# Seven products from the fourth pair on, and refilled stage borders, in a two-layer hybrid decoder trunk

## Chip, cores and metric

One Trainium2 chip, one core. The metric is the device time of one execution in microseconds (us), median of several runs.

## What is computed

The trunk has two layers. In each, x is normalized (RMSNorm), goes through a mixer (gated DeltaNet in layer 0, GLA in layer 1) and is added back, then through a gated feed-forward with a causal convolution of three taps, all in float32. The change is in the feed-forward and at its borders:

```python
D_MODEL, SEQ, D_FF, FFN_CONV = 1024, 1024, 2816, 3

def conv_glu_ffn(h, w_up, conv_w, w_down):
    u = causal_depthwise_conv(h @ w_up, conv_w)
    gate, val = jnp.split(u, 2, axis=-1)
    return (jax.nn.silu(gate) * val) @ w_down

for layer in range(2):
    hn = rms_norm(x, mix_pre_norm[layer])
    m = ...
    x = x + rms_norm(m, mix_post_norm[layer])
    f = conv_glu_ffn(rms_norm(x, ffn_pre_norm[layer]), ffn_w_up[layer],
                     ffn_conv_w[layer], ffn_w_down[layer])
    x = x + rms_norm(f, ffn_post_norm[layer])
```

## The kernel before

Every float32 matrix is split in a high part (rounded to the type that TensorE multiplies at full rate, fp32r) and a low part (the rest). A product is three matmuls: high by high, high by low, low by high (`product3`, lines 81 to 83). ScalarE makes the high parts by a copy, GpSimd the low parts of weights by a subtraction, VectorE most low parts of activations.

**The up projection.** The 2816 hidden units are 22 tiles of 128. A pair is one gate tile and one value tile of the same units, tiles 2p and 2p+1, each 128 units by 1024 tokens. The tokens are taken in two halves, near (0 to 511) and far. The first `PLAIN` = 4 pairs are made directly: per tile 2 halves x 8 blocks of the inner dimension x 3 matmuls of 128x512. The 18 others are made by seven products of half size (Strassen's scheme in Winograd's form, `first_products` for the first such pair and `seven_products`), 7 x 4 x 3 matmuls. Their operands are sums of weight quarters (`sums`, made by GpSimd's `combine`, their lows by `low`) and of token quarters (`t1`, `t2`, `t4`, and a fourth that overwrites the far half of x's first rows; made by VectorE).

**The token sums** have eight pieces, numbered 0 to 7: `first_difference`, `second`, `fourth` for c = 0 and 1, and `third_difference` for c = 0 and 1. For each, VectorE makes the sum in two or three instructions over SBUF (lines 824 to 843), ScalarE its high part (`token_sum_high`, line 616) and VectorE its low part (`token_sum_low`, line 848). Their scratch space is the tile `kept` and `spare`, the same memory in which ScalarE later keeps products of a seven-product pair (`keep`, line 653). So the first `keep` waits for all eight lows (`s_tlo` 8). The third sum's pieces overwrite x's far half and wait for `s_b12`, the last use of those tokens.

**Order.** There is no scheduler: each engine runs its own list in program order, and semaphores tie them. Per pair, ScalarE scales the gate out of PSUM (`scaled_gate`, line 626), VectorE adds the two other taps (`conv`, lines 876 and 881), ScalarE applies silu (642) and scales the value (637), VectorE convolves it and multiplies (`activated`, 887). PE may write a PSUM tile again only when its convolution is done (`ready`). For the down projection VectorE also makes four row sums of the first two pairs' hidden units (`row_sum`, 898 to 905) in the tile `sums`; SyncE stores them, and only then (`s_rstore`) may GpSimd put weight sums there:

```python
for s in s_rstore:
    pool.wait_ge(s, 16)
for pair in range(PLAIN, FT):
    operands(pair)
```

The keep of the first product stands in ScalarE's list behind all work of the last plain pair, and the second operand's product waits for it (`s_kept` 1):

```python
pe.wait_ge(s_tlo, 6)
pe.wait_ge(s_kept, 1)
quarter_product(p, S2, chain_ps, t2_hi, t2_lo, False, False)
```

**The borders.** The mixer's end (`mixer_tail`) turns and splits the new x tile by tile; between the last tiles PE already makes the near half of the feed-forward's tile 0 (`half_product`). Then all engines meet, the stage's semaphores are cleared (`clear`, line 71), all meet again (line 72), and the feed-forward's block begins. SyncE first loads the taps, then raw tiles. The feed-forward's own end does the same towards the next mixer (`lead`), with its last down steps, norms (`m_normed`, `x_normed`), deviations and turns listed by step number.

## Time and profile before

| | |
|---|---|
| median of 3 runs | 2616.05 us |
| lowest, highest | 2615.96, 2616.66 us |
| profiled execution | 2617.55 us |
| its span on the core | 2616.1 us |
| mean granted TensorE clock | 0.993 of full |

The profile is one execution of the whole program. PE is TensorE, DVE VectorE, ACT ScalarE, POOL GpSimd, SP SyncE. An engine's name with a q is its queue. A wait is put down to the instruction whose semaphore came last. The layer 0 feed-forward lies between 794 and 1463 us, that of layer 1 from 1966 us to the end.

### The profile page before, as it was taken

How to read it: one execution, taken by the hardware profiler on the slowest of the kernel's cores; microseconds unless marked ns; L12 is line 12 of the kernel's file. 1: busy time of each engine (PE TensorE's matmuls, PEld its weight loads, DVE VectorE, ACT ScalarE, POOL GpSimd, SP SyncE). 2: the span in 40 equal slices, each digit the busy share in tenths (PEclk: the TensorE clock that was granted, in tenths of full speed). 3: DMA queues.
4: the chain of work that ended last, by engine and by line, in shares of the span. 5: the costliest groups of instructions: out<-in, count | busy, mean ns of one | idle time of the engine just before them, and what ended most of it. 6: DMA issues, size and time to landing. Idle time of an engine off the chain costs nothing. (4 is left out here: it accounts for less than half of the span.)

```text
span 2616.1 us, 34535 instructions
## 1 busy us (share of the span) xinstructions
PE 2539.9 (97%) x12557; PEld 2105.9 (80%) x12557; DVE 1645.8 (63%) x1797; ACT 1189.6 (45%) x1738; POOL 1312.4 (50%) x843
## 2 busy tenths in 40 slices
PE   7899999999899999999999899999999999999998
PEld 5788888888777788888887688788877888888887
DVE  5677666777167767667328657557457766676327
ACT  6445445545443444444446434434533444444444
POOL 2454335353502778775667111111503778785767
PEclk9999999999899999999999999999999999999999
DMA  3234444334443233324765211111523223224666
GB/s 136 61 115 138 128 124 133 84 119 118 127 144 118 77 109 98 112 93 140 235 226 192 83 35 47 32 48 35 160 104 110 90 96 114 97 101 155 220 216 217
DMA packets 123392, 313.06 MB, mean 120 GB/s; under 512 B 13473, under 2 KB 27361, under 8 KB 119937
## 3 DMA queue, kind: packets, MB, share of 16 engines
q1 hardware_dynamic: 119936, 288.31, 32.6%
q0 software_dynamic: 3328, 23.07, 4.6%
q8 instruction: 78, 1.28, 0.2%
q14 instruction: 50, 0.40, 0.0%
HBM read 247.33 MB, written 110.13 MB: 137 GB/s over the span
## 5 line engine op out<-in xcount | busy, mean ns | idle before, releaser
L527 POOL TENSOR_TENSOR f_wlo<-f_raw,f_whi 128x512 fp32r<-128x512 f32 x154 | 265.5, 1732 | 137.9 <-ACT f_whi L610 137.8
L484 POOL TENSOR_TENSOR f_wlo<-f_raw,f_whi 128x512 fp32r<-128x512 f32 (+1 forms) x122 | 198.0, 1624 | 235.5 <-ACT f_whi L579 235.5
L912 DVE TENSOR_TENSOR f_wlo<-f_raw,f_whi 128x512 fp32r<-128x512 f32 x154 | 149.5, 981 | 174.7 <-ACT f_whi L610 174.7
L610 ACT ACTIVATE f_whi<-f_raw 128x1024 fp32r<-128x1024 f32 x154 | 162.7, 1059 | 202.8 <-PE f_value L83 100.9
L484 POOL TENSOR_TENSOR f_wlo<-f_sums,f_whi 128x512 fp32r<-128x512 f32 x144 | 193.1, 1363 | 37.3 <-ACT f_whi L579 37.3
L81 PE MATMUL f_value<-x_hi,f_whi 128*128 128x512 f32 x416 | 162.9, 392 | 3.4 <-POOL f_wlo L484 1.9
L82 PE MATMUL f_value<-x_lo,f_whi 128*128 128x512 f32 x416 | 162.6, 391 | 0.0
L83 PE MATMUL f_value<-x_hi,f_wlo 128*128 128x512 f32 x416 | 162.5, 391 | 0.0
L653 ACT ACTIVATE f_kept<-f_part 128x512 f32<-128x512 f32 x108 | 64.5, 597 | 162.0 <-PE f_part L83 158.0
L2004 POOL TENSOR_TENSOR g_wlo_first<-g_raw_first,g_whi_first 128x1024 fp32r<-128x1024 f32 x15 | 36.7, 2445 | 183.2 <-ACT g_whi_first L2097 183.2
L579 ACT ACTIVATE f_whi<-f_sums 128x512 fp32r<-128x512 f32 x144 | 86.0, 623 | 89.3 <-POOL f_sums L490 89.3
L81 PE MATMUL f_value<-f_whi 128*128 128x512 f32 x308 | 120.9, 393 | 2.8 <-ACT f_acc L676 2.4
L3027 POOL TENSOR_TENSOR l_wlo<-l_raw,l_whi 128x1024 fp32r<-128x1024 f32 x12 | 29.6, 2469 | 183.5 <-ACT l_whi L3056 183.5
L83 PE MATMUL f_value<-f_whi,f_wlo 128*128 128x512 f32 x308 | 120.6, 392 | 0.0
L82 PE MATMUL f_value<-f_wlo,f_whi 128*128 128x512 f32 x308 | 120.4, 391 | 0.0
L81 PE MATMUL banks<-x_hi,g_whi_first 128*128 128x512 f32 x256 | 110.0, 430 | 3.9 <-POOL g_wlo_first L2004 3.9
L83 PE MATMUL f_part<-x_hi,f_wlo 128*128 128x512 f32 x288 | 112.5, 391 | 0.0
L82 PE MATMUL f_part<-x_lo,f_whi 128*128 128x512 f32 x288 | 112.5, 391 | 0.0
L81 PE MATMUL f_part<-x_hi,f_whi 128*128 128x512 f32 x288 | 112.5, 391 | 0.0
L81 PE MATMUL banks<-x_hi,g_whi 128*128 128x512 f32 x256 | 109.0, 426 | 0.0
L83 PE MATMUL banks<-x_hi,g_wlo_first 128*128 128x512 f32 x256 | 101.1, 395 | 0.0
L82 PE MATMUL banks<-x_lo,g_whi_first 128*128 128x512 f32 x256 | 100.9, 394 | 0.0
(566 smaller groups left out, 7814.3 us busy)
## 6 DMA issues: line engine op xcount, KB each, us to landing
f_raw<-in_ffn_w_up SPq DMA_DIRECT2D x88, 512.0 KB, 3.8
f_raw<-operands_of SPq DMA_DIRECT2D x154, 256.0 KB, 2.8
f_raw<-w_sums SPq DMA_DIRECT2D x88, 256.0 KB, 3.0
w_sums<-in_ffn_w_down POOLq DMA_DIRECT2D x28, 768.0 KB, 8.4
f_raw<-in_ffn_w_down SPq DMA_DIRECT2D x66, 256.0 KB, 4.4
operands_of<-f_hid SPq DMA_DIRECT2D x22, 512.0 KB, 2.8
w_sums<-in_ffn_w_down SPq DMA_DIRECT2D x14, 768.0 KB, 7.8
w_sums<-w_sums SPq DMA_DIRECT2D x14, 768.0 KB, 6.7
```

The source lines that it names most:

```text
L81: pe.matmul(out, w_hi, x_hi, start=first, stop=False, skip_group_check=read_between)
L82: pe.matmul(out, w_hi, x_lo, start=False, stop=False, skip_group_check=read_between)
L83: return pe.matmul(out, w_lo, x_hi, start=False, stop=last, skip_group_check=read_between)
L484: pool.tensor_tensor(part_of(w_lo, k), source, part_of(w_hi, k).bitcast(F32), ALU.subtract) \
L527: pool.tensor_tensor(step_part(w_lo, more_lo, d)[:, far], source[:, far], step_part(w_hi, more_hi, d)[:, far].bitcast(F32), ALU.subtract). ...
L579: act.activation(part_of(w_hi, k), source, ACT.Copy).then_inc(s_hi, 1)
L610: act.activation(step_part(w_hi, more_hi, d)[:, :], (raw + [last_raw])[r][:, :], ACT.Copy).then_inc(s_hi, 1)
L653: act.activation(out, chain_ps, ACT.Copy).then_inc(s_kept, 1)
L912: dve.tensor_tensor(step_part(w_lo, more_lo, d)[:, near], source[:, near], plain32(step_part(w_hi, more_hi, d)[:, near]), ALU.subtract).th ...
L2004: pool.tensor_tensor(w_lo[s][:, :], raw[s][:, :], w_hi[s][:, :].bitcast(F32), ALU.subtract) \
L3027: pool.tensor_tensor(w_lo[s][:, :], raw[s][:, :], w_hi[s][:, :].bitcast(F32), ALU.subtract) \
```

## The change

1. `PLAIN` is 3: the fourth pair of each up projection is made by seven products too. The eight pieces of the token sums are made within three plain pairs. Both pieces of the third sum now come in the last plain pair.
2. Tile 1 of each up projection: VectorE makes the low part of its far columns, at the head of its list, and GpSimd that of the near ones. Its raw load is issued ahead of the taps.
3. At the mixers' ends `half_product` is cut into pieces around the last turn, the last one behind the last turned tile. Towards the next mixer it is cut likewise, and the order of the last norms, deviations and turns is another.
4. GpSimd clears no semaphores any more; the longest runs go to SyncE first.
5. In the first mixer's end one weight's high part comes a place later.

```diff
@@ -24,7 +24,7 @@
 FFN_SLOTS = 5
-PLAIN = 4
+PLAIN = 3
 TEMP_OF = (0, 1, 2, 0, 1, 2, 0, 2)
@@ -59,7 +59,7 @@
     def clear():
-        engines = (nc.sync, nc.gpsimd, nc.scalar, nc.vector)
+        engines = (nc.sync, nc.scalar, nc.vector)
         numbers = sorted(s.num for s in made)
@@ -67,7 +67,7 @@
                 first = n
-        for n, run in enumerate(runs):
+        for n, run in enumerate(sorted(runs, key=len, reverse=True)):
             engines[n % len(engines)].sem_clear(run)
@@ -112,9 +112,10 @@
-    def half_product(self, pe):
-        pe.wait_ge(self.s_lo, 1)
-        for kt in range(KT):
+    def half_product(self, pe, tiles):
+        for kt in tiles:
+            if kt == 0:
+                pe.wait_ge(self.s_lo, 1)
             f = slice(kt * P, (kt + 1) * P)
@@ -371,6 +373,8 @@
                 sp.wait_ge(s_lo, raw_released(n - FFN_RAWS))
+            if n == FFN_RAWS + 1:
+                sp.wait_ge(s_value_low, 1)
             sp.dma_start(raw[n % FFN_RAWS][:, :], w_up[layer, n // 2 + n % 2 * FT]).then_inc(s_raw[n % FFN_RAWS], 16)
@@ -416,8 +420,9 @@
+        load(1)
         sp.dma_start(taps[:, :, :], conv_w[layer]).then_inc(s_taps, 16)
-        for n in range(1, 6):
+        for n in range(2, 6):
             load(n)
@@ -430,7 +435,7 @@
                 store_row(R_F, 1)
-            if p >= PLAIN:
+            elif p > PLAIN:
                 for kind, i in ((R_F, p // 2), (R_G, p // 2 - 1)) if p % 2 else ((R_D, p // 2 - 1), (R_S, p // 2 - 1)):
@@ -514,7 +519,10 @@
-        for n in range(1, 2 * PLAIN):
+        pool.wait_ge(s_hi, 2)
+        pool.tensor_tensor(part_of(w_lo, 1)[:, near], raw[1][:, near], part_of(w_hi, 1)[:, near].bitcast(F32),
+                           ALU.subtract).then_inc(s_lo, 1)
+        for n in range(2, 2 * PLAIN):
             low(n, raw[n % FFN_RAWS][:, :])
@@ -725,14 +733,15 @@
             elif p == 1:
-                token_sum_high(1, t2_hi[:, 0:2, :])
                 token_sum_high(2, t4_hi[:, 0:2, :])
-            elif p == 2:
                 token_sum_high(3, t1_hi[:, 2:4, :])
-                token_sum_high(4, t2_hi[:, 2:4, :])
             if p < PLAIN - 1:
...
                 high(2 * p + 3)
+                if p == 0:
+                    token_sum_high(1, t2_hi[:, 0:2, :])
+                else:
+                    token_sum_high(4, t2_hi[:, 2:4, :])
             else:
@@ -784,10 +793,10 @@
                 near_deviation(near_m)
-            near_x = {SEVENTH + 4: 0, SEVENTH + 6: 1, SEVENTH + 9: 2, FOURTH + 1: 3}.get(d)
+            near_x = {SEVENTH + 4: 0, SEVENTH + 6: 1, FOURTH: 2, FOURTH + 2: 3}.get(d)
             if near_x is not None:
                 x_deviation(near_x)
-            near_high = {SEVENTH + 8: 0, FOURTH + 2: 1, FOURTH + 3: 2, FOURTH + 4: 3}.get(d)
+            near_high = {SEVENTH + 8: 0, FOURTH + 1: 1, FOURTH + 4: 2, FOURTH + 5: 3}.get(d)
             if near_high is not None:
@@ -803,10 +812,10 @@
         far_deviation(7)
+        x_deviation(6)
         x_high(5)
-        x_deviation(6)
+        x_deviation(7)
         x_high(6)
-        x_deviation(7)
         x_high(7)
@@ -928,11 +937,10 @@
         def rows_of(q):
-            if q == PLAIN:
-                row_sum(R_F, q // 2 - 1)
             if q % 2:
                 row_sum(R_F, q // 2)
-                row_sum(R_G, q // 2 - 1)
+                if q > PLAIN:
+                    row_sum(R_G, q // 2 - 1)
             else:
@@ -988,6 +996,9 @@
+        dve.wait_ge(s_hi, 2)
+        dve.tensor_tensor(part_of(w_lo, 1)[:, far], raw[1][:, far], plain32(part_of(w_hi, 1)[:, far]), ALU.subtract) \
+            .then_inc(s_value_low, 1)
         dve.wait_ge(s_taps, 16)
@@ -995,24 +1006,23 @@
             elif p == 1:
+                fourth_low(0)
+                first_difference(1)
+                first_low(1)
+            else:
+                fourth_low(1)
+                third_difference(0)
+                third_low(0)
+                third_difference(1)
+                third_low(1)
+            conv(2 * p, gate_ps, gate)
+            if p == 0:
                 second_low(0)
                 fourth(0)
-                fourth_low(0)
-            elif p == 2:
-                first_low(1)
+            elif p == 1:
                 second(1)
...
                 fourth(1)
-            else:
-                fourth_low(1)
-                third_difference(1)
-                third_low(0)
-                third_low(1)
-            conv(2 * p, gate_ps, gate)
-            if p == 1:
-                first_difference(1)
-            if p == 2:
-                third_difference(0)
             conv(2 * p + 1, value_ps[p % 2], hid[p % 2])
@@ -1068,11 +1078,11 @@
         left_gain(7)
+        m_normed(7)
+        x_normed(6)
         x_low(5)
-        x_normed(6)
-        m_normed(7)
+        x_normed(7)
         x_low(6)
-        x_normed(7)
         x_low(7)
@@ -1087,8 +1097,10 @@
             pe.wait_ge(s_lo, n + 1)
+            if n == 1:
+                pe.wait_ge(s_value_low, 1)
             if n >= 2:
-                pe.wait_ge(s_conv, n - 1)
+                pe.wait_ge(s_conv, n - 3 if n % 2 and n > 4 else n - 1)
@@ -1220,7 +1232,7 @@
             last.then_inc(s_prod, 1)
-            t = {SEVENTH + 7: 0, FOURTH: 1, FOURTH + 1: 2, FOURTH + 3: 3}.get(d)
+            t = {SEVENTH + 7: 0, FOURTH: 1, FOURTH + 3: 2, FOURTH + 4: 3}.get(d)
             if t is not None:
@@ -1228,16 +1240,19 @@
         held(3)
+        turn(5)
         if lead is not None:
...
             lead.near_logits(pe, range(KT))
-        turn(5)
-        if lead is not None:
-            lead.half_product(pe, range(0, KT // 2))
+            lead.half_product(pe, range(0, 2))
         turn(6)
         if lead is not None:
-            lead.half_product(pe, range(KT // 2, KT))
+            lead.half_product(pe, range(2, 5))
         turn(7)
+        if lead is not None:
+            lead.half_product(pe, range(5, 6))
+            pe.wait_ge(s_free, NT)
+            lead.half_product(pe, range(6, KT))
@@ -1708,8 +1723,13 @@
             pe.wait_ge(s_free, max(place(t) for t in range(NT // 2)) + 1)
-            follows.half_product(pe)
+            follows.half_product(pe, range(0, 5))
+            pe.wait_ge(s_xn, NT)
+            follows.half_product(pe, range(5, 6))
             turn(NT - 1)
+            follows.half_product(pe, range(6, 7))
+            pe.wait_ge(s_free, NT)
+            follows.half_product(pe, range(7, 8))
@@ -2235,10 +2255,11 @@
                 else:
-                    for kt_ in range(2, 5):
+                    for kt_ in range(2, 4):
                         ScalarTail.weight(act, kt_)
...
                 if final(h):
+                    ScalarTail.weight(act, 4)
                     ScalarTail.mixed_tile(act, 0)
```

VectorE's list at the start of layer 0's block (`f_kept` and `f_spare` are the scratch, `f_t1lo` the low of the first sum, `f_gate` and `f_hid` what the convolutions write), before:

```order
L824 TENSOR_TENSOR f_kept<-x_hi 128x1024
L825 TENSOR_TENSOR f_kept<-x_lo 128x1024
L827 TENSOR_TENSOR f_kept<-f_kept 128x1024
L848 TENSOR_TENSOR f_t1lo<-f_kept,f_t1hi 128x1024
L841 TENSOR_TENSOR f_kept<-x_hi,f_kept 128x1024
L843 TENSOR_TENSOR f_kept<-f_kept,x_lo 128x1024
L876 SCALAR_TENSOR_TENSOR f_gate<-banks,f_taps,f_gate 128x1023
L881 SCALAR_TENSOR_TENSOR f_gate<-banks,f_taps,f_gate 128x1022
L876 SCALAR_TENSOR_TENSOR f_hid<-f_value,f_taps,f_hid 128x1023
L881 SCALAR_TENSOR_TENSOR f_hid<-f_value,f_taps,f_hid 128x1022
```

and in the change:

```order
L1000 TENSOR_TENSOR f_wlo<-f_raw_4201,f_whi 128x512
L833 TENSOR_TENSOR f_kept<-x_hi 128x1024
L834 TENSOR_TENSOR f_kept<-x_lo 128x1024
L836 TENSOR_TENSOR f_kept<-f_kept 128x1024
L857 TENSOR_TENSOR f_t1lo<-f_kept,f_t1hi 128x1024
L850 TENSOR_TENSOR f_kept<-x_hi,f_kept 128x1024
L852 TENSOR_TENSOR f_kept<-f_kept,x_lo 128x1024
L885 SCALAR_TENSOR_TENSOR f_gate<-banks,f_taps,f_gate 128x1023
L890 SCALAR_TENSOR_TENSOR f_gate<-banks,f_taps,f_gate 128x1022
L857 TENSOR_TENSOR f_t2lo<-f_kept,f_t2hi 128x1024
L850 TENSOR_TENSOR f_spare<-x_hi,f_kept 128x1024
L852 TENSOR_TENSOR f_spare<-f_spare,x_lo 128x1024
```

A half low of tile 1 stands at the head, and the second sum's low and the fourth sum come ahead of the value's convolution.

VectorE from the row sums on (`f_sums`) to the next convolution of a gate, before:

```order
L898 TENSOR_TENSOR f_sums<-f_hid 128x512
L900 TENSOR_TENSOR f_sums<-f_hid 128x512
L902 SCALAR_TENSOR_TENSOR f_sums<-f_sums,f_hid 128x512
L905 SCALAR_TENSOR_TENSOR f_sums<-f_sums,f_hid 128x512
L848 TENSOR_TENSOR f_t1lo<-f_kept,f_t1hi 128x1024
L841 TENSOR_TENSOR f_kept<-x_hi,f_kept 128x1024
L843 TENSOR_TENSOR f_kept<-f_kept,x_lo 128x1024
L848 TENSOR_TENSOR f_t2lo<-f_kept,f_t2hi 128x1024
L841 TENSOR_TENSOR f_spare<-x_hi,f_kept 128x1024
L843 TENSOR_TENSOR f_spare<-f_spare,x_lo 128x1024
L876 SCALAR_TENSOR_TENSOR f_gate<-banks,f_taps,f_gate 128x1023
L881 SCALAR_TENSOR_TENSOR f_gate<-banks,f_taps,f_gate 128x1022
```

and in the change:

```order
L911 SCALAR_TENSOR_TENSOR f_sums<-f_sums,f_hid 128x512
L914 SCALAR_TENSOR_TENSOR f_sums<-f_sums,f_hid 128x512
L857 TENSOR_TENSOR f_t4lo<-f_spare,f_t4hi 128x1024
L833 TENSOR_TENSOR f_kept<-x_hi 128x1024
L834 TENSOR_TENSOR f_kept<-x_lo 128x1024
L836 TENSOR_TENSOR f_kept<-f_kept 128x1024
L857 TENSOR_TENSOR x_lo<-f_kept,x_hi 128x2x512
L833 TENSOR_TENSOR f_spare<-x_hi 128x1024
L834 TENSOR_TENSOR f_kept<-x_lo 128x1024
L836 TENSOR_TENSOR f_spare<-f_spare,f_kept 128x1024
L857 TENSOR_TENSOR x_lo<-f_spare,x_hi 128x2x512
L885 SCALAR_TENSOR_TENSOR f_gate<-banks,f_taps,f_gate 128x1023
```

Before, a whole plain pair, the fourth, still follows these rows. In the change the rows (from the third row sum on) are the last plain pair's, with the seventh and the eighth piece (lows into `x_lo`) ahead of its convolution.

ScalarE in the change from the highs of the first seven-product pair's operands (`f_whi`) to the copy of its first product (the last row):

```order
L587 ACTIVATE f_whi<-f_raw_4203 128x512
L587 ACTIVATE f_whi<-f_sums 128x512 x2
L624 ACTIVATE f_t4hi<-f_spare 128x1024
L624 ACTIVATE x_hi<-f_kept 128x2x512
L624 ACTIVATE x_hi<-f_spare 128x2x512
L587 ACTIVATE f_whi<-f_raw_4203 128x512
L587 ACTIVATE f_whi<-f_sums 128x512
L587 ACTIVATE f_whi<-f_raw_4202 128x512
L634 ACTIVATE f_gate<-banks,f_taps 128x1024
L650 ACTIVATE f_gate<-f_gate 128x1024
L645 ACTIVATE f_hid<-f_value,f_taps 128x1024
L661 ACTIVATE f_kept<-f_part 128x512
```

The row sums' storage, two weight sums and all three last token sums are ahead of that copy; before, this list is the same but for its place, one pair later.

## Rows read from the trace of the kernel before

**Rows 1.** The page of the kernel before, part 1: engine, busy us, share of span, instructions.
```profile
PE 2539.9 (97%) x12557; PEld 2105.9 (80%) x12557; DVE 1645.8 (63%) x1797; ACT 1189.6 (45%) x1738; POOL 1312.4 (50%) x843
```

**Rows 2.** A window of 100 us in layer 0's up projection; columns as named in the first row.
```profile
core 0: us, PE busy (x) PEld busy (x) DVE busy (x) ACT busy (x) POOL busy (x), PEclk, DMA share, GB/s
900.00:1000.00 100.00, 100.00 (x440) 82.38 (x439) 66.88 (x59) 47.28 (x71) 79.69 (x59) 1.00 0.31 103
```

**Rows 3.** The waits of PE over the whole span: us in total, times, longest us.
```profile
PE banks L81 <- PEq L72: 5.1, 2, 2.7
PE g_pm L2744 <- ACT g_vb L2200: 6.4, 1, 6.4
PE f_value L81 <- DVE f_hid L881: 1.5, 2, 0.8
```

**Rows 4.** PE's timeline: start us, us, engine, line, operation, out<-in, count [idle before <-releaser].
```profile
794.24 0.47 PE L81 MATMUL banks<-x_hi,f_whi 128*128 128x512 f32 x1 [2.73 <-PEq L72]
...
802.21 0.50 PE L81 MATMUL f_value<-x_hi,f_whi 128*128 128x512 f32 x1 [0.59 <-POOL f_wlo L484]
...
813.23 0.39 PE L81 MATMUL banks<-x_hi,f_whi 128*128 128x512 f32 x1
...
885.99 0.39 PE L81 MATMUL f_part<-f_t2hi,f_whi 128*128 128x512 f32 x1
...
1966.34 0.76 PE L81 MATMUL banks<-x_hi,f_whi 128*128 128x512 f32 x1 [2.40 <-PEq L72]
...
2058.70 0.39 PE L81 MATMUL f_part<-f_t2hi,f_whi 128*128 128x512 f32 x1
```

**Rows 5.** PE matmuls of line 82, layer 0: duration ns min/median/max, first and last start us.
```profile
L82 PE MATMUL f_part<-f_t2lo,f_whi x72: 389/389/398, 886.2 to 1211.5; 128*128 128x512 f32 x72
```

**Rows 6.** VectorE's timeline at the start of layer 0's up projection, columns as in Rows 4.
```profile
796.21 1.22 DVE L824 TENSOR_TENSOR f_kept<-x_hi 128x1024 f32<-128x1024 f32 x1 [3.18 <-DMA f_taps<-in_ffn_conv_w]
...
803.33 3.28 DVE L841 TENSOR_TENSOR f_kept<-x_hi,f_kept 128x1024 f32<-128x1024 f32 x1
806.68 3.30 DVE L843 TENSOR_TENSOR f_kept<-f_kept,x_lo 128x1024 f32<-128x1024 f32 x1
810.07 1.28 DVE L876 SCALAR_TENSOR_TENSOR f_gate<-banks,f_taps,f_gate 128x1023 f32<-128x1023 f32 x1
...
840.93 0.69 DVE L898 TENSOR_TENSOR f_sums<-f_hid 128x512 f32<-128x512 f32 x1
```

**Rows 7.** GpSimd's timeline there, and one row of VectorE beside a working GpSimd.
```profile
799.43 9.47 POOL L484 TENSOR_TENSOR f_wlo<-f_raw,f_whi 128x1024 fp32r<-128x1024 f32 x3 [20.65 <-ACT f_whi L579]
...
815.83 2.42 POOL L484 TENSOR_TENSOR f_wlo<-f_raw,f_whi 128x1024 fp32r<-128x1024 f32 x1 [6.94 <-ACT f_whi L579]
...
879.00 1.32 POOL L490 TENSOR_TENSOR f_sums<-f_raw 128x512 f32<-128x512 f32 x1
...
885.96 1.62 DVE L898 TENSOR_TENSOR f_spare<-f_hid 128x512 f32<-128x512 f32 x1
```

**Rows 8.** ScalarE's timeline in both layers.
```profile
798.28 1.06 ACT L579 ACTIVATE f_whi<-f_raw 128x1024 fp32r<-128x1024 f32 x1 [6.08 <-DMA f_raw<-in_ffn_w_up]
...
883.47 0.60 ACT L653 ACTIVATE f_kept<-f_part 128x512 f32<-128x512 f32 x1 [1.60 <-PE f_part L83]
...
1971.28 1.06 ACT L579 ACTIVATE f_whi<-f_raw 128x1024 fp32r<-128x1024 f32 x1 [6.71 <-DMA f_raw<-in_ffn_w_up]
```

**Rows 9.** DMA issues: KB each, median us from issue to landing.
```profile
operands_of<-f_sums SPq DMA_DIRECT2D x8, 256.0 KB, 2.6
```

**Rows 10.** A stretch of the first mixer, behind its longest wait of PE, columns as in Rows 2.
```profile
669.00:679.00 10.00, 7.56 (x29) 6.84 (x30) 0.29 (x1) 5.29 (x12) 6.19 (x3) 0.50 1.12 349
```

**Rows 11.** A semaphore clear at the end of the first mixer, in ns.
```profile
L71 POOLq EVENT_SEMAPHORE_RANGE_CLEAR  x1: 616/616/616, 793.3 to 793.3; - x1
```

**Rows 12.** The waits of PE at the end of layer 0's feed-forward.
```profile
PE f_value L1205 <- DVE f_xs L979: 3.1, 3, 1.3
PE f_value L81 <- ACT f_acc L676: 2.4, 1, 2.4
```

More of the change, by code:

```diff
@@ L1050, in _ @@
             near_m = {SEVENTH + 3: 0, SEVENTH + 5: 1, SEVENTH + 8: 2, FOURTH: 3}.get(d)
-            near_x = {SEVENTH + 5: 0, SEVENTH + 7: 1, SEVENTH + 10: 2, FOURTH + 2: 3}.get(d)
+            near_x = {SEVENTH + 5: 0, SEVENTH + 7: 1, FOURTH + 1: 2, FOURTH + 3: 3}.get(d)
             if near_x is not None:
@@ L1055, in _ @@
                 m_normed(near_m)
-            near_low = {SEVENTH + 9: 0, FOURTH + 3: 1, FOURTH + 4: 2, FOURTH + 5: 3}.get(d)
+            near_low = {SEVENTH + 9: 0, FOURTH + 2: 1, FOURTH + 5: 2, FOURTH + 6: 3}.get(d)
             if near_low is not None:
```

1 line of the change is left out of this document (added).

## The prediction

> **What bounds the kernel now.** I read the page first. PE is busy for 2539.9 us of a span of 2616.1 [rows 1], so PE sets the time, and inside an up projection a window shows it at 100.00 of 100.00 us with VectorE at 67 and GpSimd at 80 [rows 2]. Then I read PE's waits. What is not PE work is short: 5.1 us at two block ends, 1.5 us behind the convolutions [rows 3]. So a removed matmul is worth its spacing, and everything else costs nothing until it makes PE wait. The question is therefore whether the other engines' chains, which the change packs into fewer pairs, still end before PE needs them. For that I read the timelines of VectorE, GpSimd and ScalarE at the start of layer 0's up projection [rows 6 to 8].
>
> **What the change removes.** A pair of tiles by plain products is 96 matmuls, by seven products 84. Tile 1 takes PE from 802.21 to 813.23, 48 matmuls in 11.0 us, 0.23 each [rows 4]. Twelve fewer are 2.7 us per layer, 5.5 us in the two. A pair by seven products takes 19.0 us: its third product starts at 886.2 in the first of 18 pairs and in the last about 2 us before 1211.5, so 323.2/17 [rows 5].
>
> **What it adds: a longer chain on VectorE.** Times from here are after PE's entry into the block, 794.24 in layer 0 [rows 4]. Now the token sums begin at +2.0 (796.21), before the first raw tile's high part at +4.0 (798.28) [rows 6, 8]. In the change VectorE must first make half of tile 1's low part, so it begins behind that high part. The load is issued 0.35 us earlier, so the copy runs from about +3.8 to +4.9.
>
> How long an instruction takes beside GpSimd is the main thing to read. The difference of line 841 took 3.28 us and the addition of line 843 3.30, both while GpSimd had three lows in hand, 9.47 us from 799.43 [rows 6, 7]. A VectorE instruction of that width with GpSimd idle took 1.22 (the first of rows 6), a low alone 2.42 [rows 7]. These fit taking turns: 2.4 for GpSimd's and then 1.2 for VectorE's, and three lows with two foreign instructions between are 3 x 2.4 + 2 x 1.2 = 9.6. The convolution at 810.07, which reads PSUM, took its 1.28. I work with turns.
>
> *To the first convolution.* VectorE's half low ends at +5.6, GpSimd's half (1.3) waits for it and ends at +6.9, so PE starts tile 1 at +6.95, against +8.0 now. Then VectorE's first sum instruction 1.2, GpSimd's low of tile 2 2.4, two more instructions 2.4, the high part on ScalarE 1.15, the low of the sum 1.2, line 841 1.2, GpSimd's low of tile 3 2.4, line 843 1.2, the convolution in two instructions 2.7: 15.9 us, and the convolution ends at +22.8. PE has finished tile 1 at +18.0 and waits 4.8 us for it, since the gate's PSUM is free only then. Now it enters tile 2 at +19.0 (813.23) [rows 4].
>
> *To the row sums.* VectorE has no pause left: 15 wide instructions at 1.23 are 18.5, six of convolutions at 1.33 8.0, four row sums 2.9 (0.69 each [rows 6]), two ScalarE steps 2.3, one turn of GpSimd 0.6. That is 32.3, so they end at +55.
>
> *To the second weight sum's high part.* GpSimd may write its sums buffer only when all four row sums are stored: about 2.6 us from issue to landing [rows 9], +57.5. Its two weight sums take 1.3 each [rows 7], +60.1. ScalarE has the highs of this pair's first three operands queued ahead of the high part of the sixth token sum, which so ends at +61.9. Before, the row sums were stored a full pair ahead of that.
>
> *To the kept product.* VectorE has the low of the sixth sum and the three instructions of the seventh, each in turn with one of GpSimd's five 1.3 us instructions: 4 x 2.5 = 10.0, +71.8. ScalarE's high 1.1, low 1.2, the eighth sum 3.7, high 1.1, low 1.2: +80.1. The three highs queued on ScalarE and the scaled gate end at +81.2, the convolution at +83.9, the activation and the scaled value at +85.9, and only then, in ScalarE's order, comes the copy of the first product out of PSUM (0.60 [rows 8]), at +86.6. The second operand's product needs it. PE would be there at +72.3 and waits 14 us.
>
> **The sum.** Now that product (its S2) starts at 885.99, +91.75; in the change at +86.6, with one seven-product pair more behind it, 19.0. So layer 0's up projection ends 86.6 + 19.0 - 91.75 = 13.9 us later. In layer 1 the raw tile's copy starts at +4.9 (1971.28 against 1966.34), the chain ends at +87.4, and S2 is now at +92.4 (2058.70) [rows 4, 8]: 14.0 us. The 5.5 us of removed matmuls are inside these two numbers.
>
> The block's entry: three matmuls are held behind the last turned tile, 3 x 0.23 + 0.39, about 0.9 after latencies, and the clear on GpSimd (0.62 us [rows 11]) moves to queues whose instruction is short, worth 0.4. I take +0.5 per layer, between -0.4 and +0.9.
>
> The clock: in the first mixer, behind the wait of 6.4 us [rows 3], a full 10 us show a granted clock of 0.50, the 1.2 GHz level [rows 10]. A 14 us wait will be followed by some of that. Ten us of work at half speed would cost 5 us, none costs 0; I take 2.5 per layer. After the first wait it costs nothing, as PE waits again anyway.
>
> The end of layer 0's feed-forward: PE waits 3.1 and 2.4 us there [rows 12]. The turns, deviations and norms are reordered, and the last products of the next mixer's first tile are spread over the last turns. I take -2.5, about half, with bounds -5.5 and +5.5, as a new wait of the same size could come. The final clear is worth 0.1. Everything else moved (which down step lies in which slot, the store of the second R_F row sum) is covered by a busy PE; if it were not, it would show as PE waits between 1230 and 1400.
>
> Sum: 13.9 + 14.0 + 1.0 + 5.0 - 2.5 - 0.1 = +31.3 us. The profiled execution took 2617.55, 1.5 above the median of 2616.05; I add to the median: 2647.3.
>
> **A rule weighed.** Rows 6 and 7 alone leave two readings: turns, or a slowing by 3.28/1.22 = 2.7 for as long as GpSimd works. The second makes the four instructions to +71.8 last 13 us in place of 10. The Trainium skill (SBUF — State Buffer, Who interferes with whom) states that VectorE with two SBUF inputs and GpSimd hold one port pair as an exclusive lock for a whole instruction. By that rule the sum is the 31.3 above. By a slowing it would be some 3 us more per layer, about 2653.
>
> **Rivals.**
> - *The chains fit (faster).* If VectorE, GpSimd and ScalarE end every link before PE comes, only the gain is left: -5.5 for matmuls, -1 each at tile 1, -2.5 at the layer's end: 2606. It decides at +18.0 and +72: the convolution and the kept product must be there. For it: PE hides all of this now, with 1.5 us of waits. Against it: the convolution already ends 0.5 us before PE comes (812.71 by the row at 810.07), and begins 3 us later in the change. 7%.
> - *Little contention.* Without GpSimd's turns the chain loses 1.2 + 2.4 + 2.4 + 0.6 + 5 = 11.6 us and S2 starts at +75: 2.3 us later per layer by the same sum. 2616 + 31.3 - 23.2 = 2624. Against it are the 3.28 us instructions. 8%.
> - *The clock stays low.* If PE works ten us at the half level behind the wait and the layer's end gains nothing: +5 + 2.5, 2655. 12%.
> - *The wait takes another shape*, a step late that I hold to be covered, in either direction: 4%.
>
> **How the numbers follow.** The forecast, two waits per layer of about 5 and 14 us, gets 69%. Slower by over 0.2% (5.2 us, about what a measurement of this kernel can tell from no change) holds in it, in two rivals and most of the last: 0.91. Faster 0.07, within 0.2% 0.02. The range reaches up to the low clock, 2656, and down to 2632, which takes in chains 4 us shorter per layer and the end's larger gain; it leaves out the first two rivals.
>
> **What would show it.** PE's waits get two large rows per layer: one at tile 2 behind the gate's convolution (near 5 us), one at the first t2 product behind the copy of the first product (near 14 us); VectorE shows no pause over 1.2 us between the first low and the row sums; GpSimd's first weight sum starts about 3 us behind the last row sum. Wrong would be: the first t2 product without a wait, a first convolution ending before +19, or wide VectorE instructions of 1.2 us beside a working GpSimd.

## Result, and the profile after

| | before | changed |
|---|---|---|
| median | 2616.36 us (4 runs, 2615.96 to 2617.92) | 2639.56 us (4 runs, 2639.16 to 2640.9) |
| ratio, 95% interval | 1 | 1.0085 [1.0073, 1.0097] |
| profiled execution, its span | 2617.55, 2616.1 us | 2639.93, 2638.4 us |

The change makes the kernel 23.2 us slower; forecast were 31.3, that is 2647.3 us within 2632 to 2656, and 2639.56 lies in that range. PE's busy time on the page after answers to [rows 1]:

```profile
span 2638.4 us, 34563 instructions
PE 2541.6 (96%) x12533; PEld 2105.1 (80%) x12533; DVE 1655.5 (63%) x1807; ACT 1197.9 (45%) x1754; POOL 1328.1 (50%) x861
```

The 24 matmuls are gone from the count (12557 to 12533), but PE's busy time rose by 1.7 us: some of what is left ran at half clock, as the windows below show behind the t2 product's wait. The waits of PE over the whole span, after (the groups of [rows 3]):

```profile
PE f_part L81 <- issue: 23.8, 2, 12.3
PE banks L81 <- DVE f_gate L890: 8.4, 2, 4.4
PE g_pm L2765 <- ACT g_vb L2220: 2.3, 1, 2.3
PE banks L81 <- PEq L72: 1.5, 2, 0.8
```

There are two new waits per layer, as forecast: about 4 us at the third tile behind the gate's convolution, and about 12 us at the first t2 product. The last two groups shrank, from 6.4 and 5.1. PE's timeline after, at the same places as [rows 4]:

```profile
797.99 0.50 PE L81 MATMUL f_value<-x_hi,f_whi 128*128 128x512 f32 x1 [0.93 <-POOL f_wlo L523]
813.60 0.48 PE L81 MATMUL banks<-x_hi,f_whi 128*128 128x512 f32 x1 [4.40 <-DVE f_gate L890]
...
864.41 0.39 PE L83 MATMUL f_value<-f_t1hi,f_wlo 128*128 128x512 f32 x1
877.06 0.77 PE L81 MATMUL f_part<-f_t2hi,f_whi 128*128 128x512 f32 x1 [12.26 <-issue]
877.62 0.63 PE L82 MATMUL f_part<-f_t2lo,f_whi 128*128 128x512 f32 x1
...
882.26 0.40 PE L81 MATMUL f_value<-x_hi,f_whi 128*128 128x512 f32 x1
```

PE's first matmul in the block is at 791.22, and times marked + count from there (in the table below they count from the release of the barrier at line 72, 0.1 us earlier, so the same t2 product stands there at +86.0). Tile 1 starts at +6.8, tile 2 at +22.4, PE is there for the t2 product at +73.6 and starts it at +85.8. "issue" names no releaser for that wait. ScalarE's timeline names it (start us, us, engine, line, operation):

```profile
874.41 1.06 ACT L650 ACTIVATE f_gate<-f_gate 128x1024 f32<-128x1024 f32 x1 [2.72 <-DVE f_gate L890]
875.37 1.10 ACT L645 ACTIVATE f_hid<-f_value,f_taps 128x1024 f32<-128x1024 f32 x1
876.37 0.59 ACT L661 ACTIVATE f_kept<-f_part 128x512 f32<-128x512 f32 x1
```

The copy of the first product out of PSUM ends at 876.96, and PE goes on at 877.06. The chain behind it, VectorE's and then GpSimd's timeline (it answers to [rows 6, 7]):

```profile
796.10 0.69 DVE L1000 TENSOR_TENSOR f_wlo<-f_raw,f_whi 128x512 fp32r<-128x512 f32 x1 [6.10 <-ACT f_whi L587]
796.89 2.13 DVE L833 TENSOR_TENSOR f_kept<-x_hi 128x1024 f32<-128x1024 f32 x1
798.94 3.44 DVE L834 TENSOR_TENSOR f_kept<-x_lo 128x1024 f32<-128x1024 f32 x1
...
845.53 0.69 DVE L914 SCALAR_TENSOR_TENSOR f_sums<-f_sums,f_hid 128x512 f32<-128x512 f32 x1
853.27 1.95 DVE L857 TENSOR_TENSOR f_t4lo<-f_spare,f_t4hi 128x1024 fp32r<-128x1024 f32 x1 [7.05 <-ACT f_t4hi L624]
855.30 2.14 DVE L833 TENSOR_TENSOR f_kept<-x_hi 128x1024 f32<-128x1024 f32 x1
857.37 2.33 DVE L834 TENSOR_TENSOR f_kept<-x_lo 128x1024 f32<-128x1024 f32 x1
859.77 2.17 DVE L836 TENSOR_TENSOR f_kept<-f_kept 128x1024 f32<-128x1024 f32 x1
```

```profile
796.16 1.77 POOL L523 TENSOR_TENSOR f_wlo<-f_raw,f_whi 128x512 fp32r<-128x512 f32 x1 [20.41 <-ACT f_whi L587]
797.90 3.40 POOL L489 TENSOR_TENSOR f_wlo<-f_raw,f_whi 128x1024 fp32r<-128x1024 f32 x1
806.81 2.83 POOL L489 TENSOR_TENSOR f_wlo<-f_raw,f_whi 128x1024 fp32r<-128x1024 f32 x1 [5.51 <-ACT f_whi L587]
848.92 1.31 POOL L495 TENSOR_TENSOR f_sums<-f_raw 128x512 f32<-128x512 f32 x1 [17.25 <-DMA operands_of<-f_sums]
```

The last row sum ends at 846.22 (+55.0), GpSimd's first weight sum starts 2.7 us later, and VectorE stands 7.05 us for a high part on ScalarE.

The time by stage of the profiled executions, us, from the same timelines (an entry is the release of the barrier at line 72; "up" ends with the first matmul of line 82 into f_value in the down projection):

| kernel | to entry 0 | up 0 | down 0 | mixer 1 | up 1 | down 1, end | t2 product at, layers 0 and 1 | span |
|---|---|---|---|---|---|---|---|---|
| before | 794.1 | 431.8 | 236.8 | 503.5 | 432.4 | 217.5 | +91.9, +92.5 | 2616.1 |
| changed | 791.1 | 447.4 | 232.8 | 502.9 | 446.5 | 217.7 | +86.0, +86.0 | 2638.4 |
| e_borders | 790.7 | 431.7 | 233.0 | 502.8 | 433.1 | 217.6 | +91.8, +93.2 | 2608.9 |
| e_weight_later | 791.4 | 433.3 | 236.9 | 503.5 | 432.2 | 217.6 | +93.4, +92.3 | 2614.9 |
| e_half_low_only | 796.3 | 435.6 | 236.8 | 503.6 | 435.9 | 217.8 | +95.7, +96.0 | 2626.0 |
| e_no_half_low | 790.8 | 443.2 | 233.2 | 501.9 | 442.8 | 217.6 | +82.2, +82.1 | 2629.5 |
| e_sum_high_first | 791.3 | 443.0 | 232.9 | 501.2 | 443.0 | 217.6 | +81.8, +81.4 | 2629.0 |
| e_keep_first | 791.3 | 444.4 | 231.7 | 502.1 | 446.1 | 217.7 | +79.9, +80.0 | 2633.3 |
| e_all_three | 793.0 | 436.5 | 233.1 | 502.0 | 437.8 | 217.6 | +72.0, +71.7 | 2620.0 |
| e_pool_waits | 792.3 | 445.2 | 233.0 | 502.0 | 445.8 | 217.6 | +84.9, +85.1 | 2635.9 |
| e_filled | 790.8 | 445.5 | 231.9 | 502.4 | 445.0 | 217.6 | +86.4, +85.9 | 2633.2 |
| e_borders_early_weight | 792.2 | 433.3 | 233.1 | 501.3 | 433.5 | 217.5 | +93.4, +93.6 | 2610.9 |
| e_clear_only | 789.1 | 431.7 | 237.0 | 503.0 | 431.9 | 217.4 | +91.7, +92.0 | 2610.1 |

Changed against before: -3.0, +15.6, -4.0, -0.6, +14.1, +0.2, together +22.3, the difference of the spans. The up projections lose 29.7 us, the border at the end of layer 0's feed-forward gives 4 back. One number of the table needs care: what comes before entry 0 ends anywhere from 789.1 to 796.3, in kernels that are all but equal there. The medians of the kernel before in the three sets of runs below are 2617.74, 2617.12 and 2617.21, their single runs from 2611.9 to 2621.5. The changed kernel was measured only in the first set, beside a kernel before of 2616.36. So where a median below is set against its 2639.56, 1 us or so can come from the sets; the stages of the table carry the argument.

### The profile page after: what moved, and what is told of

Read it like the earlier page. It is cut to its first block and busy times, and to the rows that moved or that the text cites. A ratio compares the mean times of both kernels' runs of the same rounds, so it can differ in the third digit from the quotient of the medians.

```text
span 2638.4 us, 34563 instructions
## 1 busy us (share of the span) xinstructions
PE 2541.6 (96%) x12533; PEld 2105.1 (80%) x12533; DVE 1655.5 (63%) x1807; ACT 1197.9 (45%) x1754; POOL 1328.1 (50%) x861
## 3 DMA queue, kind: packets, MB, share of 16 engines
q8 instruction: 78, 1.28, 0.2%
## 5 line engine op out<-in xcount | busy, mean ns | idle before, releaser
L489 POOL TENSOR_TENSOR f_wlo<-f_raw,f_whi 128x512 fp32r<-128x512 f32 (+1 forms) x122 | 186.6, 1529 | 171.0 <-ACT f_whi L587 170.8
L489 POOL TENSOR_TENSOR f_wlo<-f_sums,f_whi 128x512 fp32r<-128x512 f32 x152 | 205.7, 1376 | 38.6 <-ACT f_whi L587 38.6
L81 PE MATMUL f_value<-x_hi,f_whi 128*128 128x512 f32 x400 | 156.4, 391 | 0.9 <-POOL f_wlo L523 0.9
L82 PE MATMUL f_value<-x_lo,f_whi 128*128 128x512 f32 x400 | 156.3, 391 | 0.0
L83 PE MATMUL f_value<-x_hi,f_wlo 128*128 128x512 f32 x400 | 156.2, 391 | 0.0
L83 PE MATMUL f_part<-x_hi,f_wlo 128*128 128x512 f32 x304 | 118.7, 391 | 0.0
L82 PE MATMUL f_part<-x_lo,f_whi 128*128 128x512 f32 x304 | 118.7, 391 | 0.0
L81 PE MATMUL f_part<-x_hi,f_whi 128*128 128x512 f32 x304 | 118.7, 390 | 0.0
```

The source lines that it names most:

```text
L81: pe.matmul(out, w_hi, x_hi, start=first, stop=False, skip_group_check=read_between)
L82: pe.matmul(out, w_hi, x_lo, start=False, stop=False, skip_group_check=read_between)
L83: return pe.matmul(out, w_lo, x_hi, start=False, stop=last, skip_group_check=read_between)
L489: pool.tensor_tensor(part_of(w_lo, k), source, part_of(w_hi, k).bitcast(F32), ALU.subtract) \
```

## Experiments

**The borders alone.** The kernel before, with the change's edits at the stages' borders and in the first mixer, nothing of the up projection; the core of it:

```
-        engines = (nc.sync, nc.gpsimd, nc.scalar, nc.vector)
+        engines = (nc.sync, nc.scalar, nc.vector)
...
-            near_x = {SEVENTH + 4: 0, SEVENTH + 6: 1, SEVENTH + 9: 2, FOURTH + 1: 3}.get(d)
+            near_x = {SEVENTH + 4: 0, SEVENTH + 6: 1, FOURTH: 2, FOURTH + 2: 3}.get(d)
...
-            lead.half_product(pe, range(KT // 2, KT))
+            lead.half_product(pe, range(2, 5))
```

> The kernel before with the refilled borders, the clears and the later weight copy of the change, but four plain pairs and tile 1 as before. Theory (the loss is all in the up projections' chains, the borders pay): the stages outside the up projections keep what the changed kernel shows for them, -3.0 us up to layer 0's entry, -4.0 at layer 0's end, -0.6 in layer 1's mixer: 2608 to 2609. Rival (the borders only shift PE's work behind the barriers, the gain came with the later phase): 2614 to 2617.

Measured: 2612.55 us (10 runs), ratio 0.9985 [0.9975, 0.9995], above the 2608 to 2609 expected, which counted in the 3.0 us before entry 0. All of the loss lies in the up projections, and the borders alone beat both kernels. PE's waits from 1180 to 1470 us in this kernel, against 3.1, 2.4 and 2.3 before ([rows 12]; the last is the next block's entry):

```profile
PE f_value L81 <- DVE f_wlo L913: 1.9, 3, 0.8
PE f_value L1206 <- DVE f_xs L980: 0.9, 2, 0.5
PE f_value L1206 <- DVE f_acc L980: 0.9, 1, 0.9
PE l_pm L88 <- PEq L72: 0.8, 1, 0.8
```

**One border edit at a time.** e_weight_later is the kernel before with only the weight's high part a place later in the first mixer:

```
-                    for kt_ in range(2, 5):
+                    for kt_ in range(2, 4):
                         ScalarTail.weight(act, kt_)
                 scale_values(h)
                 if final(h):
+                    ScalarTail.weight(act, 4)
```

> The kernel before with one weight's high part a place later in the first mixer's last head, nothing else. Theory (that copy stood ahead of the values' scaling in ScalarE's list, and PE waited for the values): the wait on g_vb falls from 6.4 to near 2.3 us, the block of layer 0 begins 3 to 4 us earlier: about 2612.5. Rival (the wait varies by itself, or the gain came from the clears and held matmuls): 2616, the wait still near 6.4.

Measured: 2617.03 us, 1.0000 [0.9990, 1.0009]: no change. The wait for g_vb fell to 2.3 us as the theory had it, and the total stayed as the rival had it. In its profile the entry came 2.7 us earlier and the up projection took 1.5 more. e_borders_early_weight is e_borders without that edit:

> The kernel before, with the change's edits at the stages' borders alone and without the one in the first mixer (the weight's high part stays where it was). Theory (the 3 us that layer 0's up projection began earlier in the changed kernel come from that weight's high part, whose place shortened PE's wait for g_vb from 6.4 to 2.3): the entry into layer 0 is back at 793.5 to 794.3, the wait for g_vb back at 6.4, the end of layer 0's feed-forward still 3.5 to 4 us shorter, total 2614 to 2616 against 2612.5 with that edit. Rival (the earlier entry comes from the products spread over the last turns and from the clears): the entry stays at 790.5 to 791.5 and the total at 2612.5.

Measured: 2612.34 us (11 runs), 0.9982 [0.9973, 0.9991], not 2614 to 2616: the total of the rival. The wait for g_vb was back at 6.5 and yet the entry lay at 792.2, between what the two had for it. And e_clear_only, the kernel before with the clears alone (the first lines of the diff above, and the sorted runs):

> The kernel before, with the clears of the semaphores taken off GpSimd and given to SyncE, ScalarE and VectorE, the longest run first. Theory (the clear of 0.62 us on GpSimd is what the barrier at each of the four stage borders waits for): each border 0.3 to 0.6 us shorter in the profile, 1 to 2 us in all, total 2614.5 to 2616. Rival (the barrier waits for something else, as PE's own last instructions): no stage moves by over 0.1 us, total within 0.5 us of the kernel before.

Measured: 2617.03 us, 1.0000 [0.9991, 1.0009]; behind entry 0 the stages lie within 0.2 us of before, but layer 1's mixer and up projection 0.5 shorter each. For the total the rival holds. The clears do shorten PE's wait behind the barrier at the ends of the two mixers, from 2.73 to 2.34 us and from 2.40 to 2.14 (together 5.1 to 4.5), and not the one at the end of layer 0's feed-forward (2.32 and 2.31). This kernel, whose first mixer is but for the clears the one before, shows the wait for g_vb at 3.9 and its entry at 789.1:

```profile
PE banks L81 <- PEq L72: 4.5, 2, 2.3
PE g_pm L2744 <- ACT g_vb L2200: 3.9, 1, 3.9
```

So that wait goes up and down by itself, and the 3.0 us before entry 0 in the changed kernel are not shown to be an effect of any edit. Of the borders, the reordered norms, turns and spread products at the end of layer 0's feed-forward are what is worth 4 us: all kernels that have them show 231.7 to 233.2 there, all others 236.8 to 237.0.

**The half low part alone.** The kernel before (four plain pairs) with the second item only, tile 1's low part half on VectorE ahead of the token sums:

```
+        dve.wait_ge(s_hi, 2)
+        dve.tensor_tensor(part_of(w_lo, 1)[:, far], raw[1][:, far], plain32(part_of(w_hi, 1)[:, far]), ALU.subtract) \
+            .then_inc(s_value_low, 1)
         dve.wait_ge(s_taps, 16)
         first_difference(0)
```

> The kernel before, four plain pairs, with tile 1's low part halved between VectorE and GpSimd and its load ahead of the taps (and the looser wait of tile 5). Theory (it delays VectorE's list by some 4 us from the first instruction): tile 1 starts 1.0 us earlier, but PE waits about 4.4 us at tile 2 for the gate's convolution, in both layers; the later chain has slack, so 2.5 to 4 us per layer with the clock: 2621 to 2625. Rival (the earlier tile 1 is a gain, the delay is absorbed): 2614.

Measured: 2624.95 us, 1.0031 [1.0019, 1.0044]. Its up projections are 3.8 and 3.5 us longer, and PE waits for the gate's convolution:

```profile
PE banks L81 <- DVE f_gate L888: 9.2, 4, 4.3
PE banks L81 <- PEq L72: 5.1, 2, 2.7
```

**The change without it.** The changed kernel with GpSimd making tile 1's low part whole (the lines above taken out, and the loop from 1 again):

> The changed kernel with tile 1's low part whole on GpSimd and the taps first, as before. Theory (VectorE's list runs without a pause from the block's entry to the kept product, so what is taken off its head comes off the end): tile 2 has no wait over 0.5 us, the t2 product starts about 3.3 us earlier per layer although tile 1 starts 1 us later: 2631 to 2634. Rival (the late product waits for stored row sums or weights by a clock of their own, not for VectorE's list): 2639 to 2642.

Measured: 2631.76 us, 1.0063 [1.0046, 1.0080]. The t2 product is 3.8 us earlier in both layers, about as much as the half low part cost alone. The wait for the first gate convolution is gone, and the one at the t2 product is 13.7 in place of 12.3: PE comes there some 5 us earlier, and the chain ends 3.8 earlier. The half low part, meant to let PE begin tile 1 sooner, delays the chain that PE then waits for, and costs 8 us of the 23 (the up projections are 4.2 and 3.7 us shorter without it).

**ScalarE's order.** In the changed kernel, the last token sum's high part ahead of the seventh pair's high operands:

```
             else:
+                token_sum_high(5, t4_hi[:, 2:4, :])
                 high_operands(PLAIN, A11, S1, S2)
...
             else:
-                token_sum_high(5, t4_hi[:, 2:4, :])
                 for c in range(2):
```

> The changed kernel, with one step of ScalarE moved: in the last plain pair the high part of the last token sum comes ahead of the four high operands of the seventh pair, not behind them. Theory (a chain over ScalarE, VectorE and GpSimd sets the start of the first t2 product): VectorE's low of that sum waited 7.05 us for ScalarE in the changed kernel; it comes some 4.5 us earlier, and the two turned differences, the last low parts, the convolution, the copy and the product move with it: PE's two long waits shrink from 12.3 and 11.5 to about 7.5 each, the t2 product starts at about +81.5 behind the entry in place of +86.0, and the total is 8 to 9 us lower, near 2631. Rival (the wait for the weight sums' transfer on GpSimd, 17.25 us of idle time there, is what PE waits for in the end): the t2 product stays at +86 and the total at 2639.5, within 1 us.

Measured: 2630.89 us, 1.0053 [1.0037, 1.0070], 8.7 less than the changed kernel; its up projections are 4.4 and 3.5 us shorter. VectorE's low part comes with no idle time before it, 6.55 us earlier; GpSimd still idles until the row sums are stored:

```profile
846.72 1.22 DVE L857 TENSOR_TENSOR f_t4lo<-f_spare,f_t4hi 128x1024 fp32r<-128x1024 f32 x1
...
855.43 1.95 DVE L857 TENSOR_TENSOR x_lo<-f_kept,x_hi 128x1024 fp32r<-128x1024 f32 x1 [2.80 <-ACT x_hi L624]
```

```profile
849.50 2.05 POOL L495 TENSOR_TENSOR f_sums<-f_raw 128x512 f32<-128x512 f32 x1 [17.28 <-DMA operands_of<-f_sums]
```

The idle time of 17 us on GpSimd is no wait of PE's; it mattered because a high part that has nothing to do with the weight sums stood behind them on ScalarE. Of the 6.55 us, 2.80 come back at the next high part, which is now the one queued behind a weight sum.

**The copy first.** The copy of the first product ahead of the last plain pair's scaled gate:

```
                 high_operands(PLAIN, A12, S3, A22)
+                keep(PLAIN, 0)
                 scaled_gate(p)
...
             more = p < FT - 1
-            keep(p, 0)
+            if p > PLAIN:
+                keep(p, 0)
```

> The changed kernel, with the copy of the first seven-product pair's first product put on ScalarE ahead of the last plain pair's scaled gate, not behind the SiLU of its last tile. Theory (PE's long wait ends with this copy, and the copy stands behind the last convolutions on its engine only by its place in the program): the wait shrinks from 12.3 to about 6.5 and the first t2 product starts at +80 to +81, but the copies and convolutions of the pair are still late, so PE then waits about 3 us at each of the next two t2 products, and the total is within 3 us of the changed kernel's 2639.5. Rival (only the first t2 product is late, the rest of the pair has slack): no later waits, and the total is 10 to 11 us lower, near 2629.

Measured: 2636.96 us, 1.0077 [1.0061, 1.0094]. PE's waits from 790 to 905 us:

```profile
PE f_part L81 <- DVE x_lo L859: 6.5, 1, 6.5
PE banks L81 <- DVE f_gate L892: 4.3, 1, 4.3
PE f_part L81 <- ACT f_kept L661: 2.2, 1, 2.2
```

The t2 product starts 6 us earlier and the wait is halved, as expected, but in layer 0 half of it and in layer 1 nearly all is lost again by the end of the stage (444.4 and 446.1 us against 447.4 and 446.5). A wait taken off its first place comes back at the next product of the same chain, and with it the low clock: in layer 1 PE waits 0.9 and 2.2 us at the two next products into f_part, and the 6 us behind the second wait (2066 to 2072) were granted 0.66 and 0.77, an estimated 1.7 us more.

**All three.** The last three edits of the changed kernel together:

> Three edits of the changed kernel together: no half low part of tile 1 on VectorE (GpSimd makes it whole, as in the kernel before, and the three pairs of token sums stay), the last token sum's high part ahead of the seventh pair's high operands, and the first copy ahead of the last plain pair's scaled gate. Theory (the chain is one sum of links, and each edit takes its own): the first t2 product starts at +73 to +74, PE's waits in the up projection are about 4.7 at the first gate convolution, 3 to 5 at the first t2 product and 3 at the next, some 11 us a layer with no half-clock stretch, the 5.5 us of removed matmuls and the 4 to 5 us of the borders show, and the total is 2616 to 2621. Rival (with the chain shortened the product waits for the weight sums, through GpSimd's combines and the load of the sums): the t2 product doesn't start before +80 whatever is edited, and the total stays at 2628 or above.

Measured: 2619.62 us, 1.0008 [0.9998, 1.0018]; t2 products at +72.0 and +71.7. The theory's number holds, 14 us a layer off the t2 product by three edits of ScalarE's, VectorE's and GpSimd's order. The wait of 4.7 us at the first gate convolution, which the theory still counted on, did not come; the half clock, which it held to be gone, did (last section). What is left in layer 0 are short waits:

```profile
PE f_part L81 <- ACT f_kept L654: 2.2, 1, 2.2
PE f_value L81 <- POOL f_wlo L485: 2.2, 1, 2.2
PE f_part L81 <- DVE x_lo L852: 1.9, 1, 1.9
```

With the half clock behind them they still cost more than the removed matmuls give: the up projections are 4.7 and 5.4 us longer than before. With the borders' 5 us in it, this kernel is no faster than the kernel before and 7 us behind e_borders.

**One turn taken away.** The changed kernel, with a wait on GpSimd for VectorE's first difference of token tiles:

```
+        pool.wait_ge(s_t, 1)
         for n in range(2, 2 * PLAIN):
             low(n, raw[n % FFN_RAWS][:, :])
```

> The changed kernel, with one wait added: GpSimd begins the low part of tile 2 only when VectorE's first token difference is done, so that in the stretch between the half low part and tile 3's low no turn of GpSimd falls on that difference. Theory of turns (a wide VectorE instruction takes 1.2 us alone, and behind a GpSimd instruction of 2.4 us that many more): the difference takes 1.2 to 1.3 us in place of 3.44, the low part of tile 2 starts as much later and its turn falls on the next VectorE instruction in place of that one, so the first gate convolution ends no more than 1.1 us earlier (+21 to +22.2), and the total moves by 0 to -2 us. Rival (each overlap costs on its own, and a turn avoided is a turn saved): the convolution ends 2.2 us earlier and the t2 product too, in both layers, total near 2635.

Measured: 2637.57 us, 1.0078 [1.0061, 1.0095], 2.0 below the changed kernel. VectorE's timeline at the start of layer 0's up projection, then GpSimd's:

```profile
800.06 1.21 DVE L835 TENSOR_TENSOR f_kept<-x_lo 128x1024 f32<-128x1024 f32 x1
801.35 1.23 DVE L837 TENSOR_TENSOR f_kept<-f_kept 128x1024 f32<-128x1024 f32 x1
803.71 2.46 DVE L858 TENSOR_TENSOR f_t1lo<-f_kept,f_t1hi 128x1024 fp32r<-128x1024 f32 x1 [1.13 <-ACT f_t1hi L625]
806.25 3.28 DVE L851 TENSOR_TENSOR f_kept<-x_hi,f_kept 128x1024 f32<-128x1024 f32 x1
809.61 1.23 DVE L853 TENSOR_TENSOR f_kept<-f_kept,x_lo 128x1024 f32<-128x1024 f32 x1
```

```profile
802.66 2.42 POOL L489 TENSOR_TENSOR f_wlo<-f_raw,f_whi 128x1024 fp32r<-128x1024 f32 x1 [3.60 <-DVE f_kept L837]
805.70 2.75 POOL L489 TENSOR_TENSOR f_wlo<-f_raw,f_whi 128x1024 fp32r<-128x1024 f32 x1 [0.62 <-ACT f_whi L588]
```

Line 835's instruction took 1.21 us in place of 3.44 (line 834 in the changed kernel), and the last three of these took 2.46, 3.28 and 1.23 where they had taken 1.23, 1.23 and 3.29. With GpSimd idle the wide instruction takes 1.2, and a turn avoided is for the most part moved: the t2 product came 1.1 and 0.9 us earlier, as by turns, not 2.2. The ends tell turns from a slowing: GpSimd's two instructions end at 805.08 and 808.45, VectorE's beside them at 806.17 and 809.53, 1.09 and 1.08 us later, little less than the 1.22 that one takes alone. By a slowing of 2.7 for the time of the overlap (1.37 and 2.20 us) the two would have lasted 2.1 and 2.6 us, by an estimate from these rows, not 2.46 and 3.28.

**PE kept busy in its wait.** Four times the same twelve matmuls into a bank that is overwritten later, between the S1 and the S2 product:

```
+            for _ in range(4):
+                for kt in range(KT // 2):
+                    product3(pe, value[:, near], x_hi[:, KT // 2 + kt, 0:P], x_hi[:, KT // 2 + kt, P:2 * P],
+                             x_hi[:, KT // 2 + kt, near], x_lo[:, KT // 2 + kt, near], kt == 0, kt == KT // 2 - 1)
             pe.wait_ge(s_tlo, 6)
```

> The changed kernel, with PE kept at work in its long wait: 48 further matmuls of 512 columns, whose sums go to a PSUM bank that the next product but one overwrites, stand between the S1 and the S2 product of the first seven-product pair of each layer (11.0 us at 0.23 each, of waits of 12.3 and 11.5). Nothing that is used is computed otherwise. Theory (the t2 product's own 12 matmuls took 5.4 and 4.4 us at a granted clock of 0.50 because PE had stood idle, and that is the clock's whole price): the first t2 product still starts at +86, its 12 matmuls take 2.8 to 3.0 us at clock 1.00, and the total is 3.5 to 4.5 us lower, near 2635.5. Rival (the slow start is the product's own, by its operands' late arrival or by the reads of VectorE's fresh tiles, not the clock): its 12 matmuls take over 4 us again and the total doesn't move, or rises by what the added matmuls delay, 0 to 2 us.

Measured: 2637.32 us, 1.0078 [1.0062, 1.0093], 2.2 below the changed kernel (3.1 if each is counted from the kernel before of its own set) where 3.5 to 4.5 were expected; the two intervals overlap, so the total by itself decides nothing. The profile does. Windows of the changed kernel around its t2 product (PE idle, then starting at 877.06), and of this one (columns as in [rows 2]; the granted clock is the number before the last two):

```profile
870.10:877.10 7.00, 0.04 (x1) 0.07 (x1) 3.45 (x4) 4.28 (x7) 6.40 (x5) 0.50 0.29 90
877.10:880.10 3.00, 3.00 (x7) 2.41 (x8) 2.83 (x3) 1.93 (x4) 2.55 (x3) 0.50 0.34 141
880.10:883.10 3.00, 3.00 (x10) 2.36 (x9) 2.67 (x2) 0.60 (x1) 3.00 (x2) 0.65 0.23 87
```

```profile
870.00:875.00 5.00, 5.00 (x23) 4.13 (x23) 3.14 (x3) 2.28 (x4) 5.00 (x4) 1.00 0.00 0
875.00:878.00 3.00, 2.30 (x10) 1.61 (x9) 1.28 (x1) 3.00 (x5) 2.06 (x3) 1.00 0.90 284
878.00:881.00 3.00, 3.00 (x15) 2.44 (x14) 2.85 (x2) 1.82 (x4) 3.00 (x3) 1.00 0.16 66
```

The first matmul of the t2 product starts at 877.24, 0.4 us later behind the entry than in the changed kernel, and the last of the twelve at 879.86: 2.85 us with its spacing, against 5.20 (877.06 to 882.26). The up projections are 1.9 and 1.5 us shorter; from the t2 product to their end they take 359.1 us in both layers in place of 361.4 and 360.5. The clock, and not the operands, made the slow start, and its price is 2.3 and 1.4 us, 3.7 for both layers.

## Why the prediction was right, and where its sizes were off

**The two waits.** Right in place, in cause and nearly in size. The convolution that lets PE into tile 2 ended at +22.2 (forecast +22.8) and the wait was 4.4 (4.8); the row sums ended at +55.0 (+55); the last of the seventh sum's differences at +70.7 (861.94; forecast +71.8); the copy at +85.7 and the t2 product at +85.8 (+86.6). VectorE's longest pause ahead of the row sums was 1.13 us (forecast: none over 1.2). That this chain sets the product is shown by e_no_half_low, e_sum_high_first, e_keep_first and e_all_three: each moved it by what the removed link is worth (3.8, 4.2, 6.1 and 14.0 us).

**The up projections' terms.** The added pair was priced at 19.0 us from [rows 5], and that reading is off: the t2 product is the third of the first such pair, but the second of every later one. From 902.50 to 1209.19, sixteen pairs apart, it is 19.2 us a pair. With that, the t2 product at +86.0 and +91.9 before, layer 0's term is 13.3 in place of 13.9. Layer 1's term of 14.0 was 12.7 (+92.5 before): the step that failed is "in layer 1 the raw tile's copy starts at +4.9", the difference to layer 0 carried over from [rows 8]. Raw tile 1 is loaded first of all now, and its high part ends in both layers alike; the half low parts on VectorE start at +4.9 in layer 0 and at +4.9 in layer 1 (1979.16 behind 1974.26).

**The clock.** 2.5 us a layer were taken between 0 and 5. Measured by e_filled, 2.3 and 1.4; the twelve matmuls alone show 2.35 in layer 0 and 1.4 in layer 1 (4.22 us against 2.85, 2060.22 to 2064.44). The mechanism was right, the size 1.3 too large in sum. Behind the first wait, at tile 2, the clock fell as well (0.55 over the 3 us from 813.6), and PE only waited that much less at the t2 product, as forecast.

**The entries.** The term of +1.0 had the wrong sign. Its smaller part was right in size: the clear taken off GpSimd, "worth 0.4", shortens the wait behind the barrier (PEq L72) by 0.39 and 0.26 us in e_clear_only, too little for its total to show. The part that failed is the held matmuls: priced at "about 0.9 after latencies", they fill this wait in place of lengthening the block. It fell to 0.80 and 0.75 us with them, and mixer 1, which ends at the second entry, took 501.2 to 502.9 us in the kernels with the spread products and 503.0 to 503.6 in those without.

**The end of layer 0's feed-forward.** -2.5 were taken between -5.5 and +5.5, -4.0 came, and -3.6 to -5.1 in all the kernels that have those edits. In place of the waits of 3.1 and 2.4 [rows 12] the changed kernel has 1.9, 0.9 and 0.4, 2.3 less, and the wait behind the barrier there fell from 2.3 to 0.8, 1.5 less: together 3.8 of the 4.0.

**What the sum left out.** The edit in the first mixer was held to be covered. It is: e_weight_later measured 1.0000 and e_borders is not faster with it than without. The -3.0 us of the profile before entry 0 can't be told from the difference between two executions: nearly the same instructions gave 789.1 there once, and by their medians e_borders and e_borders_early_weight are 5.2 and 4.9 us below the kernel before, of which 3.8 and 3.7 lie at the end of layer 0's feed-forward.

The terms as measured are 13.3 + 12.7 + 3.7 - 4.0 - 3.0 - 0.4 (mixer 1 and the end) = 22.3, the difference between the spans. Of the 9.0 us from there to the forecast of 31.3, 1.9 are the two chains, 1.3 the clock, 1.6 the entries (+1.0 against the -0.6 of mixer 1), 1.5 the end of layer 0 and 3.0 what varies before entry 0; the end of the program took 0.3 off. So 6.0 us are the sum's own error, and nearly every term of it erred towards a longer time.

**The rivals.** "The chains fit" is refuted by the wait of 12.3 us at the t2 product and that of 4.4 at tile 2. Little contention, S2 at +75: it is what e_all_three reaches by order alone, but in the changed kernel the wide instructions beside GpSimd took 2.13 to 3.44 us, and the seventh sum's took 2.14, 2.33 and 2.17, between 2.5 by turns and 1.23 with none. The Trainium skill (SBUF — State Buffer, Who interferes with whom) calls the contention for the port pair that VectorE and GpSimd share an exclusive lock. e_pool_waits agrees: VectorE's instruction ends 1.08 us behind GpSimd's, and one instruction's 2.2 us moved to its neighbours and left the sum 1.1 us shorter. The prediction's row of a convolution that keeps its 1.28 us shows nothing about turns, as GpSimd's lows had ended at 808.90 when it began at 810.07; but all 88 convolutions of line 876 in the kernel before took 1.28 to 1.29 us, with GpSimd busy for 80% of the stretch of [rows 2]. "The clock stays low" counted ten us of work at half speed a layer; the trace shows 5.2 and 4.2 us of it at most, and the end of layer 0 gained.

## What to carry to other kernels

PE is what counts only as long as its operands come; before a tile's worth of products is taken off PE, add up the chain on the other engines to the first product that needs it, with the turns between VectorE and GpSimd in it, and ask which instruction stands behind another's wait only by its place in the program. Here 12 matmuls fewer a layer stand for 2.7 us of PE, and one high part queued behind an unrelated weight sum cost 4.2. And an edit bundled with others should be run alone: two of the bundle did nothing that a total shows, one cost 8 us, and the reordered border was worth keeping, as e_borders, 0.15% faster than the kernel before.
